# Units of seven block products: high and low halves of the tokens in one matmul of 512 columns, joined when a bank is read

## What is computed

```
hn = rms_norm(concat(meta, x))
xa, sa, vb, gb, sb, ma, mb = split(hn @ w_in)         # w_in: 2048 x 14336
ya = rg_lru(conv4(xa)) * silu(sa);       pa = ya @ w_proj_a
yb = silu(layer_norm(conv31(vb * sigmoid(gb)))) * silu(sb);   pb = yb @ w_proj_b
h  = h + (sigmoid(ma) * pa + sigmoid(mb) * pb) @ w_out
out = rms_norm(h)[16:]
```

## Time and profile before

| | us |
|---|---|
| median of 3 runs | 1776.68 (1776.1 to 1776.89) |
| the profiled execution | 1777.52 |
| its span | 1775.7 |
| TensorE busy in it | 1754.6 (99%) |
| VectorE, ScalarE, POOL busy | 1255.2, 839.8, 298.0 |
| chain that ended last: L793 (the units) | 39% of the span |
| L886 (branches), L753 (plain products), L980 and L994 (output) | 28%, 16%, 10% |

### The profile page before, as it was taken

One profiled execution on the slowest core, in us unless ns is written; L12 is line 12 of the kernel. 1 busy time (PEld: TensorE's weight loads), 2 busy tenths in 40 slices (PEclk: granted clock), 3 DMA queues, 4 the chain that ended last, 5 costly groups with the idle time before them and its releaser, 6 DMA issues.

```text
span 1775.7 us, 30385 instructions
## 1 busy us (share of the span) xinstructions
PE 1754.6 (99%) x12812; PEld 1672.8 (94%) x12812; DVE 1255.2 (71%) x1489; ACT 839.8 (47%) x1142; POOL 298.0 (17%) x331
## 2 busy tenths in 40 slices
PE   9899999999999999999999999999999999999998
PEld 8899999999999988999999999999888899997886
DVE  7969988888888898777767667787633286764431
ACT  6556556455564523455555444555422154443322
POOL 0502222222122101111111111221100111120000
PEclk9999999999999999999999999999999999999999
DMA  6247867668677565777765767685767689757422
GB/s 207 88 125 157 189 162 172 154 150 182 156 162 167 137 184 166 190 208 220 205 173 156 191 167 203 179 214 165 234 213 243 174 213 202 178 139 265 154 83 95
DMA packets 285671, 311.80 MB, mean 176 GB/s; under 512 B 9440, under 2 KB 239968, under 8 KB 284384
## 3 DMA queue, kind: packets, MB, share of 16 engines
q1 hardware_dynamic: 211024, 188.21, 33.6%
q0 software_dynamic: 74512, 121.65, 31.6%
HBM read 235.38 MB, written 45.09 MB: 158 GB/s over the span
## 4 chain that ended last, share of the span: by engine, by line
PE 92%; DVE 3%; DMA 2%; ACT 1%; issue 1%; SPq 0%; POOL 0%; DVEq 0%; POOLq 0%; ACTq 0%
PE psum L793 39%; PE psum L886 28%; PE psum L753 16%; PE psum L980 7%; PE psum L994 3%; PE psum L853 1%; DMA t_lo<-m_spill 1%; DVE region L1914 1%; DMA raw<-in_w_proj_a 1%; DMA region<-in_x_channels 1%; DVE region L1545 0%; DVE w_lo L1699 0%; DVE t_lo L1830 0%; DVE total L1587 0%; DVE c_lo L1560 0%
## 5 line engine op out<-in xcount | busy, mean ns | idle before, releaser
L1224 ACT ACTIVATE w_hi<-raw 128x1024 fp32r<-128x1024 f32 x110 | 116.2, 1057 | 286.6 <-PE psum L753 134.7
L1479 DVE SCALAR_TENSOR_TENSOR region<-region,params 128x512 f32<-128x512 f32 x368 | 250.4, 743 | 0.0
L1699 DVE TENSOR_TENSOR w_lo<-raw,w_hi 128x1024 fp32r<-128x1024 f32 x110 | 134.7, 1226 | 131.7 <-ACT w_hi L1224 131.6
L1706 DVE TENSOR_TENSOR w_lo<-region,w_hi 128x1024 fp32r<-128x1024 f32 x108 | 132.2, 1224 | 103.0 <-ACT w_hi L1240 102.8
L1706 DVE TENSOR_TENSOR x_lo<-region,x_hi 128x1024 fp32r<-128x1024 f32 x108 | 132.0, 1224 | 89.8 <-ACT x_hi L1240 87.9
L886 PE MATMUL psum<-x_hi,w_hi 128*128 128x264 f32 x896 | 181.9, 284 | 0.0
L886 PE MATMUL psum<-x_lo,w_hi 128*128 128x264 f32 x896 | 181.9, 284 | 0.0
L793 PE MATMUL psum<-t_hi,w_hi 128*128 128x256 f32 x576 | 142.0, 285 | 0.0
L793 PE MATMUL psum<-t_lo,w_hi 128*128 128x256 f32 x576 | 141.3, 284 | 0.0
L793 PE MATMUL psum<-t_hi,x_hi 128*128 128x256 f32 x576 | 139.4, 281 | 0.9 <-ACT aux L1282 0.9
L793 PE MATMUL psum<-t_lo,x_hi 128*128 128x256 f32 x576 | 139.2, 281 | 0.0
(11 more groups left out here) (249 smaller groups left out, 4484.2 us busy)
## 6 DMA issues: line engine op xcount, KB each, us to landing
raw<-in_w_in SPq DMA_DIRECT2D x112, 512.0 KB, 4.0
region<-in_w_in SPq DMA_DIRECT2D x56, 1024.0 KB, 7.1
wide<-region POOLq DMA_DIRECT2D x98, 256.0 KB, 4.9
region<-in_w_proj_b SPq DMA_DIRECT2D x16, 1024.0 KB, 9.3
raw<-in_w_out SPq DMA_DIRECT2D x32, 512.0 KB, 3.7
raw<-in_w_proj_a SPq DMA_DIRECT2D x31, 512.0 KB, 4.2
region<-in_w_in POOLq DMA_DIRECT2D x28, 512.0 KB, 7.2
sigmoid_spill<-wide POOLq DMA_DIRECT2D x16, 512.0 KB, 5.4
```

Source lines behind the costliest of these rows:

```text
L1224: act.activation(cut_at(n)[0], raw_at(n).rearrange("p (k n) -> p k n", k=4), ACT.Copy).then_inc(hi_ready, 1)
L1479: ins = dve.scalar_tensor_tensor(conv_b[:, t, :], moved, w, conv_b[:, t, :], ALU.mult, ALU.add)
L1699: dve.tensor_tensor(lo, raw_at(n).rearrange("p (k n) -> p k n", k=4), hi.bitcast(F32), ALU.subtract).then_inc(lo_ready, 1)
L1706: dve.tensor_tensor(lo, operand_source(v, q).rearrange("p (r h) n -> p r h n", h=2), hi.bitcast(F32), ALU.subtract).then_inc(lo_ready, 1)
```

## The change

The token halves move into common tensors, `x_parts` and `t_parts`, with an axis of two for high and low. In the units, the pass with the high weights is one matmul per step: 512 columns, of which the first 256 are the high half of the tokens and the second 256 the low half, written to both halves of the bank. The pass with the low weights adds to the first half of the bank only. A block product is then the sum of the two halves of its bank. The seed, `u2` and `u3` are read at full width (512), c22 and c12 are made at full width in place, in `u3` and `u2`, and VectorE joins the halves: `join_rest` adds the two halves of `u2` and of `u3` into the slot, and `join_first` adds the first halves of banks 0 and 1 to the second halves, which ScalarE has copied to the slot (`copy_first`). The gate is one operation over the whole slot (`gate`). The normalisation of the B branch keeps its places in the program. The other products (`multiply`, `item`) stay as they are; only their names of the tensors change.

The diff, without the declarations of semaphores, the waits of TensorE and POOL that only change name, and the views:

```diff
@@ -129,4 +129,5 @@
-        x_hi, x_lo = sb("x_hi", [P, CT, T], F32R), sb("x_lo", [P, CT, T], F32R)
-        t_hi, t_lo = sb("t_hi", [P, 4, KH, HS], F32R), sb("t_lo", [P, 4, KH, HS], F32R)
+        x_parts, t_parts = sb("x_parts", [P, 2, CT, T], F32R), sb("t_parts", [P, 2, 4, KH, HS], F32R)
+        x_hi, x_lo = (x_parts[:, n] for n in range(2))
+        t_hi, t_lo = (t_parts[:, n] for n in range(2))
         y_hi, y_lo = (t[:, :, :, :].rearrange("p b j n -> p (b j n)").rearrange("p (k s) -> p k s", k=CT)
@@ -188,5 +189,5 @@
-        aux = sb("aux", [P, 2 * HS + 2 * SEQ])
-        u2, u3 = (aux[:, n * HS:(n + 1) * HS] for n in range(2))
-        ln = aux[:, 2 * HS:].rearrange("p (t s) -> p t s", t=2)
+        aux = sb("aux", [P, 4 * SEQ])
+        u2, u3 = (aux[:, n * SEQ:(n + 1) * SEQ] for n in range(2))
+        ln = aux[:, 2 * SEQ:].rearrange("p (t s) -> p t s", t=2)
...
@@ -382,2 +384,9 @@
+        def token_parts(q):
+
+            if q in (A11, A12, S4):
+                k, t = (0 if q == A11 else KH), META + (HS if q == S4 else 0)
+                return x_parts[:, :, k:k + KH, t:t + HS]
+            return t_parts[:, :, {S1: T_N1, S2: T_T2, S3: T_T3, A22: T_T4}[q]]
+
         def spilled_block(q):
@@ -599,5 +608,2 @@
                     pool.wait_ge(o_gated, w)
-                    if w >= STD:
-                        pool.wait_ge(c11_ready, w - STD + 1)
-                        pool.wait_ge(c21_ready, w - STD + 1)
                     pool.dma_start(pair_rows(spill[kind], i), o).then_inc(done, 16)
@@ -785,3 +791,3 @@
                 hi, lo = cut_slots(slot(n))
-                operand = token_operand(q)
+                parts = token_parts(q)
                 if v == NX:
@@ -789,14 +795,11 @@
-                def passes(weights, parts, first, last):
-                    for k in range(KH):
-                        for part in parts:
-                            ins = pe.matmul(psum[:, bank, 0:HS], weights[:, k // 2, k % 2, :], operand[part][:, k, :],
-                                            start=first and k == 0 and part == 0, stop=last and k == KH - 1,
-                                            skip_group_check=more)
-                    return ins
-
                 pe.wait_ge(hi_ready, n + 1)
-                passes(hi, (0, 1), not more, False)
+                for k in range(KH):
+                    pe.matmul(psum[:, bank, :].rearrange("p (a n) -> p a n", a=2), hi[:, k // 2, k % 2, :],
+                              parts[:, :, k, :], start=not more and k == 0, stop=False, skip_group_check=True)
                 pe.wait_ge(lo_ready, n + 1)
-                passes(lo, (0,), False, True).then_inc(multiplied, 1)
+                for k in range(KH):
+                    last = pe.matmul(psum[:, bank, 0:HS], lo[:, k // 2, k % 2, :], parts[:, 0, k, :],
+                                     start=False, stop=k == KH - 1, skip_group_check=True)
+                last.then_inc(multiplied, 1)
...
@@ -1256,6 +1257,6 @@
             def bank(v, n):
-                return psum[:, 3 * (w_of(v) % 2) + n, 0:HS]
+                return psum[:, 3 * (w_of(v) % 2) + n, :]
             def gate_of(v):
-                return {MA: ACT.Sigmoid, MB: ACT.Sigmoid, SA: ACT.Silu, SB: ACT.Silu, PB: ACT.Copy}[w_of(v) // PAIRS]
+                return {MA: ACT.Sigmoid, MB: ACT.Sigmoid, SA: ACT.Silu, SB: ACT.Silu}[w_of(v) // PAIRS]
@@ -1269,2 +1270,4 @@
                     act.wait_ge(p_ready, PAIRS - 1 + v - NX)
+                else:
+                    act.wait_ge(first_ready, v - 1)
                 act.activation(bank(v, 1), bank(v, 0), ACT.Copy, scale=-1.0).then_inc(seeded, 1)
@@ -1274,3 +1277,3 @@
                 act.wait_ge(multiplied, chunk(v, S2) + 1)
-                wait(act, c12_ready, v)
+                wait(act, rest_ready, v)
                 act.activation(u2, bank(v, 1), ACT.Copy, scale=-1.0).then_inc(u2_ready, 1)
@@ -1280,13 +1283,6 @@
                 act.wait_ge(multiplied, chunk(v, S3) + 1)
-                wait(act, c22_ready, v)
+                wait(act, rest_ready, v)
                 act.activation(u3, bank(v, 1), ACT.Copy).then_inc(u3_ready, 1)
-            def gate_c11(v):
-
-                w = w_of(v)
-                act.wait_ge(multiplied, chunk(v, A12) + 1)
-                wait(act, o_spilled[w % 2], spills(w))
-                act.activation(o_slots[:, w % 2, 0, 0:HS], bank(v, 0), gate_of(v)).then_inc(c11_ready, 1)
-
-            def gate_c21(v):
+            def copy_first(v):
@@ -1295,6 +1291,6 @@
                 wait(act, o_spilled[w % 2], spills(w))
-                act.activation(o_slots[:, w % 2, 1, 0:HS], bank(v, 1), gate_of(v)).then_inc(c21_ready, 1)
-
-            def gate_rest(v):
+                b = 3 * (w % 2)
+                act.activation(o_slots[:, w % 2, :, 0:HS], psum[:, b:b + 2, HS:], ACT.Copy).then_inc(first_copied, 1)
+            def gate(v):
@@ -1302,7 +1298,6 @@
                 if w < PA * PAIRS:
-                    act.wait_ge(c22_ready, v + 1)
-                    act.wait_ge(c12_ready, v + 1)
-                    rest = o_slots[:, w % 2, :, HS:]
+                    act.wait_ge(first_ready, v + 1)
+                    act.wait_ge(rest_ready, v + 1)
                     done = {MA: o_gated, MB: o_gated, SA: sa_silu, SB: sb_silu}[w // PAIRS]
-                    act.activation(rest, rest, gate_of(v)).then_inc(done, 1)
+                    act.activation(o_slots[:, w % 2], o_slots[:, w % 2], gate_of(v)).then_inc(done, 1)
@@ -1334,6 +1329,6 @@
                     if p == 2 and follows:
-                        gate_c21(v - 1)
+                        copy_first(v - 1)
                     if p == 4:
                         if follows:
-                            gate_rest(v - 1)
+                            gate(v - 1)
                         if 2 <= v < PAIRS + 2:
@@ -1344,4 +1339,2 @@
                             silu_ln(w_of(v) - SB * PAIRS - 1)
-                    if p == 6:
-                        gate_c11(v)
                     if v == PAIRS + 3 and p == 3:
@@ -1396,5 +1389,5 @@
                 if m == 0:
-                    gate_c21(NX - 1)
+                    copy_first(NX - 1)
                 if m == 2:
-                    gate_rest(NX - 1)
+                    gate(NX - 1)
                     silu_ln(PAIRS - 1)
@@ -1407,2 +1400,3 @@
             read_u3(NV - 1)
+            copy_first(NV - 1)
@@ -1424,4 +1418,2 @@
                     .then_inc(hi_ready, 1)
-                if i == 1:
-                    gate_c21(NV - 1)
                 if i < 2:
@@ -1732,12 +1724,7 @@
-            def bank(v, n):
-                return psum[:, 3 * (w_of(v) % 2) + n, 0:HS]
-
             def read_c22(v):
-                w = w_of(v)
                 dve.wait_ge(u3_ready, v + 1)
                 dve.wait_ge(multiplied, chunk(v, S1) + 1)
-                wait(dve, o_spilled[w % 2], spills(w))
-                dve.tensor_tensor(o_slots[:, w % 2, 1, HS:], u3, bank(v, 2), ALU.subtract).then_inc(c22_ready, 1)
+                dve.tensor_tensor(u3, u3, psum[:, 3 * (w_of(v) % 2) + 2, :], ALU.subtract).then_inc(c22_ready, 1)
@@ -1745,6 +1732,21 @@
-                w = w_of(v)
                 dve.wait_ge(multiplied, chunk(v, S4) + 1)
                 dve.wait_ge(u2_ready, v + 1)
-                dve.tensor_tensor(o_slots[:, w % 2, 0, HS:], u2, bank(v, 2), ALU.add).then_inc(c12_ready, 1)
+                dve.tensor_tensor(u2, u2, psum[:, 3 * (w_of(v) % 2) + 2, :], ALU.add).then_inc(c12_ready, 1)
+
+            def join_first(v):
+
+                first, b = o_slots[:, w_of(v) % 2, :, 0:HS], 3 * (w_of(v) % 2)
+                dve.wait_ge(first_copied, v + 1)
+                dve.tensor_tensor(first, first, psum[:, b:b + 2, 0:HS], ALU.add).then_inc(first_ready, 1)
+
+            def join_rest(v):
+
+                w = w_of(v)
+                dve.wait_ge(c12_ready, v + 1)
+                dve.wait_ge(c22_ready, v + 1)
+                wait(dve, o_spilled[w % 2], spills(w))
+                parts = aux[:, 0:2 * SEQ].rearrange("p (b a n) -> p b a n", b=2, a=2)
+                dve.tensor_tensor(o_slots[:, w % 2, :, HS:], parts[:, :, 0, :], parts[:, :, 1, :], ALU.add)\
+                    .then_inc(rest_ready, 1)
@@ -1771,4 +1773,2 @@
                 dve.wait_ge(sa_silu, i + 1)
-                dve.wait_ge(c11_ready, w - STD + 1)
-                dve.wait_ge(c21_ready, w - STD + 1)
                 dve.tensor_tensor(o_slots[:, w % 2], o_slots[:, w % 2], h_tiles, ALU.mult).then_inc(ya_ready, 1)
...
@@ -1815,3 +1813,3 @@
                 dve.wait_ge(ln_loaded, 16 * (3 * PAIRS + i + 1))
-                for done in (c11_ready, c21_ready, c12_ready):
+                for done in (first_ready, rest_ready):
                     dve.wait_ge(done, v + 1)
@@ -1841,2 +1839,4 @@
                         read_c12(v - 1)
+                        join_first(v - 1)
+                        join_rest(v - 1)
                     if q != A11:
@@ -2000,4 +2000,7 @@
```

(5 more changed lines are left out.)

15 lines of the change are left out of this document (6 added, 9 removed).

## The result

| | before | after |
|---|---|---|
| median, us | 1776.79 (1776.1 to 1777.41, 4 runs) | 1766.53 (1765.72 to 1768.35, 4 runs) |
| ratio | | 0.9943, 95% interval 0.9928 to 0.9959 |
| span of the profiled execution | 1775.7 | 1766.5 |

The change makes the kernel 0.57% faster. The forecast was 1767.7 us, range 1760.5 to 1775. The total came out close, and in part by luck: two of its terms were wrong by 3 to 4 us in opposite directions. The rest of this text is about the terms.

A forecast was written before the change was run, and what follows sets the result against it. TensorE, busy 1754.6 of 1775.7 us, was taken as the bound. Terms: 16.4 - 4.0 - 0.3 - 0.5 - 0.25 - 2.4 = 8.95 us gained, so 1768.5 us profiled, 1767.7 as a median; range 1760.5 to 1775.

The forecast's parts named there:

- Rival 3: Units: each run of 256 pays the fixed 12 ns, a pair stays at 237.3 ns; 1785.2 us, chance 0.13.
- the TensorE term: Units: one 512-column matmul replaces each pair of 256; 233 products gain 82 ns (t) or 55 ns (x), 16.4 us.
- a t operand (four of seven products): Units: a pair with a t operand gains 10.3 ns, priced from the 227.0 ns y-operand row; 82 ns per product.
- The branch loop: Units 2 to 9: convolution rows through one buffer take 20.4 us against a 19.43 us unit; TensorE waits 4.0 us.
- I take the median: Units 2 to 9: the branch rows' load lands in the median 7.6 us (5.1 shortest, 8.3 longest), giving the 4.0 us wait.
- Rival 1: Units 2 to 9: the branch loop does not bind, landings stay under 7.0 us; 1763.7 us, chance 0.22.
- Under sb: Seven units under sb: the VectorE and ScalarE loop takes 19.49 us against a unit of 19.43; 0.3 us lost.
- The end of the 28 units: Entering projection a: longer u3 copy and c22 read delay a chain with a 9.21 us load; 0.5 us lost.
- Unit 28: VectorE is behind after the operand switch; the seven products gain nothing and the longer read costs 0.25 us.
- Before the output product: Chain from c12 of unit 34 to the fifth merged load: longer reads and joins cost 1.5 and 0.9 us, together 2.4.
- the first output chunks, which were covered by that wait, stay so: Entering the output product: the first output chunks remain hidden behind the wait for the merged load, at no added cost.
- after the second only the second join stands in the way: Before the output product: after c12 of unit 35 only the second join delays gating pb; 0.9 us.

The follow-up runs named there:

- the run with other forms: Changed kernel with each product of the 28 units reading its 512 token columns in another form (one run or two, other addresses), values no longer the layer's: 1765.67 us.
- the run with both together: Changed kernel with POOL issuing the A22 addition directly ahead of the load of the convolution rows, after waiting for the same sums: 1796.02 us (ratio 1.0109).
- TensorE's half alone: Kernel before with the common tensors and 512-column matmuls, banks still read at 256 columns, low token halves left out: 1759.72 us (ratio 0.9902).
- VectorE's half alone: Changed kernel with two 256-column matmuls per step, one to each half of the bank, instead of one of 512: 1781.84 us (ratio 1.0028).
- the later copy alone: Changed kernel with the last unit's copy of first halves (and VectorE's join of them) moved behind the first output-weight chunk's cut: 1766.96 us (ratio 0.9942).
- the reordered end: Changed kernel with the last unit's first-halves copy behind the first output chunk, and VectorE's c12, second join, pb gate ahead of second merged cuts: 1763.02 us (ratio 0.9921).

## Why the prediction was right, point by point

- **The fixed part belongs to the instruction, not to the run**: right. Rival 3 falls, at 231 ns against 237.3 (its point of decision was 233), and two runs cost at most 1 ns in the run with other forms. But "hardly grows with the width" is too strong: over its columns (106.7 and 213.3 ns) an instruction takes 12 ns with 256 and 17.5 with 512, so of the 24 ns of a pair 7 are gained.
- **The size of the TensorE term, 16.4 us**: too large. Over the units the mean is 230.8 ns for 237.6 of a pair and 118.1 for 118.4 in the third pass. A product gains 56 ns, so the 233 products give 13.2 us. By kind, from the table above, a t product with weights in `w_hi` gains 90 ns, more than the 82 forecast, since its pairs took 239.9 ns and not the mean of 237.3. A t product with weights in the x tensor gains 44 and not 82, an x product 40 to 46 and not 55. The step that was mis-sized is "a t operand (four of seven products)": the row for y operands, 227.0 ns, was that of a stage where all passes are 512 wide and all weights lie in `w_hi` and `w_lo`, and half of the units' weights do not. The row beside it, 230.4, would have been right for the seven on average. As for the rule that was weighed, columns over 2.4 GHz plus 2.5 ns (the Trainium skill, TensorE: Matmul & The Clock Gate, Back-to-back issue gap), the runs do not agree: 213.3 + 2.5 is 215.8 ns, and the lowest mean of any form here is 226.6. The section gives that rule for an isolated matmul; its figure of about 131 ns at 512 columns in a stream of weight loads and matmuls is further off still.
- **The branch loop, 4.0 us**: its steps were right to a few tenths where it binds (12.35 for 12.4 us), its consequence too (the wait for u2 that one chance meeting and the run with both together show). The landing was wrong. The step that failed is "I take the median": the 7.6 us were not a property of the load but of the A22 addition 0.9 to 3.4 us ahead of it in POOL's queue. The earlier trace rows held 5.1 us beside 8.3, and the distance to the addition tells them apart. The addition waits for a block's load and moves with TensorE, the branch load waits for VectorE's sums and does not. A shorter unit and a longer loop both pull them apart: five of the eight distances are 3.2 us and more after the change against one before, with TensorE's half alone also five are 2.9 to 3.3 us, with VectorE's half alone seven are 3.4 to 3.8. The median landing falls to 5.7. Rival 1 named the outcome, and "what else is under way" was as near as it came to the cause. This term and the one above were wrong by +4.0 and -3.2 us and nearly cancelled, which is luck.
- **Under sb, 0.3 us**: 0. The loop is some 19.27, the unit 19.54. Both were off by 0.1 to 0.2. (Its own figures, 7 x 0.06, make 0.4 and not 0.3.)
- **The end of the 28 units, 0.5 us**: a gain of 1.5 instead. The load that set that end landed in 7.2 us, not 9.21. Why was not tried, and since this wait is 0 to 1.1 us in other traces, the 1.5 us may be the difference of two executions.
- **Unit 28, 0.25 us**: 0.64 us more of waits (0.34 and 0.42 against 0.12).
- **Before the output product, 2.4 us**: 2.85 in the product and 1.45 at its entry. The step that failed is "the first output chunks, which were covered by that wait, stay so". The prediction looked at VectorE and left out that ScalarE's new copy waits for A22 and stands ahead of them. The step "after the second only the second join stands in the way" failed too: the merged cuts stood there as well, delayed by that copy. The first is shown by the later copy alone (TensorE enters after 0.30 us for 1.45), both by the reordered end, which gives back 3.5 us in the time, of which a part is better order than before the change.
- **Net**: 8.95 us forecast, 10.26 measured between medians, 9.2 between the two traces.

## What to carry to other kernels

Merging two narrow matmuls into one wide one gains part of the time that an instruction takes beyond its columns, here 7 ns of 238 (5 to 10 by the places of the operands), and it does so with two separate runs as well as with one. Take both prices from rows with the same mix of widths and the same places of *both* operands.

A landing time is no constant of a transfer. Ask which transfer stands ahead of it in the same queue, and whether a change moves the two against each other.

When a step that waits for TensorE is put ahead of the first steps of the next stage on an engine, it delays all of them; here one copy of 0.6 us on ScalarE let TensorE in 1.45 us late. At the end of a stage, first what the next stage's start needs, then the copies.

## What was not expected of the hardware

- The same load lands in 4.9 us (median) when it is issued 0.7 us ahead of an addition on POOL's queue and in 9.7 us when it is issued 0.9 us behind it. The addition lands in 6.4 us (median) with the load 2.5 to 3.8 us behind it and in 9.9 us behind the load.
- Among others of its width a 512-column matmul costs 226.6 to 228 ns with both operands in `t_parts` and `w_hi` or `w_lo`, and 230.0 to 232.7 where one of them lies in `x_parts`, whose rows of 528 elements are 2112 bytes apart and used from byte 64 on. Whether the pitch or the start does it was not tried; taking x from a multiple of 2048 bytes gave 2 ns back.
- With 256-column matmuls between the wide ones, t operands and weights in `w_hi`, the wide ones cost 229.6 ns: the first of eight 233.6, the last two 226.7. Without them 227.9. Where either operand lies in `x_parts` the three kinds change by -1.4, -0.1 and +0.5 ns.
